# A decoder step on one core: HGRN2 projections and levels ahead of the attention projections

## What is computed

```python
h = rmsnorm(x, norm_mix)
hq, hf, hi, hg, nq, kc, vc, ks, vs, kw, vw, ngate, mgate = split(h @ w_in)
# HGRN2, 4 heads of 128: f = lb + (1-lb) sigmoid(hf), k = (1-lb) sigmoid(-hf)
#   S_t = f_t S_(t-1) + k_t hi_t ; o = silu(hq) S, rmsnorm, times silu(hg)
# attention, 8 heads of 64 in 2 groups:
#   compressed blocks of 32 rows + the rows themselves (selected) + a window
#   each with its own softmax, gated by sigmoid(ngate)
x += (sigmoid(g_a) * (a @ W_a) + sigmoid(g_b) * (b @ W_b)) @ w_out
h2 = rmsnorm(x, norm_ffn); g, u = split(h2 @ w_gate_up)
x += (gelu(causal_conv3(g)) * u) @ w_down
```

## Time and profile before

| | |
|---|---|
| runs | 1332.82 us median of 3 (1332.56 to 1334.46) |
| profiled execution | 1333.15 us |
| its span, first to last instruction | 1331.3 us |
| TensorE busy, share | 1252.7 us, 94% |
| VectorE, ScalarE, GpSimd busy | 652.9, 463.5, 152.4 us |
| mean granted TensorE clock | 0.966 of full |

### The profile page before, as it was taken

One profiled execution on the slowest core, in us unless ns is written; L12 is line 12 of the kernel. 1 busy time (PEld: TensorE's weight loads), 2 busy tenths in 40 slices (PEclk: granted clock), 3 DMA queues, 4 the chain that ended last, 5 costly groups with the idle time before them and its releaser, 6 DMA issues.

```text
span 1331.3 us, 20487 instructions
## 1 busy us (share of the span) xinstructions
PE 1252.7 (94%) x8353; PEld 1037.4 (78%) x8353; DVE 652.9 (49%) x1210; ACT 463.5 (35%) x788; POOL 152.4 (11%) x298
## 2 busy tenths in 40 slices
PE   5999988999998999999799999879999999999996
PEld 3567565667998999999765765656689989999994
DVE  3012476435755777653211225653475477676333
ACT  1120323435335444432112122243543454444220
POOL 0201032002110110100101012400021010110000
PEclk9999988998999999999999999889899999999998
DMA  7552422034944454333553342020566434433501
GB/s 228 206 157 93 128 64 64 1 96 116 291 141 127 129 180 136 106 133 125 159 193 95 127 136 85 9 56 6 172 179 223 131 123 159 158 111 128 180 1 39
DMA packets 136669, 166.01 MB, mean 125 GB/s; under 512 B 14612, under 2 KB 97334, under 8 KB 136246
## 3 DMA queue, kind: packets, MB, share of 16 engines
q1 hardware_dynamic: 136570, 164.64, 38.8%
HBM read 156.22 MB, written 12.46 MB: 127 GB/s over the span
## 4 chain that ended last, share of the span: by engine, by line
PE 87%; DVE 6%; issue 4%; ACT 2%; POOL 1%; DMA 0%; SPq 0%; POOLq 0%; DVEq 0%; PEldq 0%
PE mm L628 59%; PE ax L628 23%; PE ax L631 4%; ACT attb L1176 1%; POOL mixb L1957 1%; DVE ring_low L1728 1%; POOL mixb L1972 1%; DMA attb<-in_norm_final 0%; ACT work L1176 0%; DVE hT L1465 0%; DVE hT L1828 0%; DVE pcs L1583 0%; DVE attb L1591 0%; ACT work_parts L1176 0%; DVE xT L1873 0%
## 5 line engine op out<-in xcount | busy, mean ns | idle before, releaser
L1728 DVE TENSOR_TENSOR ring_low<-ring,work_parts 128x2048 fp32r<-128x2048 f32 (+1 forms) x96 | 207.2, 2158 | 143.7 <-ACT work_parts L1176 143.3
L628 PE MATMUL mm<-work_parts 128*128 128x320 f32 x832 | 258.4, 311 | 6.8 <-DVE h_low L1732 6.6
L628 PE MATMUL mm<-h_low,work_parts 128*128 128x320 f32 x832 | 260.0, 312 | 0.0
L628 PE MATMUL mm<-work_parts,ring_low 128*128 128x320 f32 x832 | 256.9, 309 | 0.0
L1176 ACT ACTIVATE work_parts<-ring 128x2048 fp32r<-128x2048 f32 (+1 forms) x96 | 173.7, 1810 | 159.5 <-PE mm L628 81.1
L628 PE MATMUL mm<-hT,ring 128*128 128x320 f32 (+1 forms) x896 | 216.7, 440 | 0.0
L628 PEld LDWEIGHTS mm<-hT,ring 128*128 128x128 f32 (+1 forms) x896 | 140.2, 177 | 70.2 <-issue 7.9
L628 PEld LDWEIGHTS mm<-work_parts 128*128 128x128 f32 x832 | 157.0, 189 | 11.3 <-issue 9.2
L628 PEld LDWEIGHTS mm<-work_parts,ring_low 128*128 128x128 f32 x832 | 157.4, 189 | 0.0
L628 PEld LDWEIGHTS mm<-h_low,work_parts 128*128 128x128 f32 x832 | 157.3, 189 | 0.0
L628 PE MATMUL ax<-act_parts,work_parts 128*128 128x320 f32 x544 | 125.8, 310 | 2.3 <-DVE ring_low L1728 1.6
(11 more groups left out here) (194 smaller groups left out, 1514.6 us busy)
## 6 DMA issues: line engine op xcount, KB each, us to landing
ring<-in_w_gate_up SPq DMA_DIRECT2D x44, 1024.0 KB, 6.8
ring<-in_w_in SPq DMA_DIRECT2D x12, 2048.0 KB, 8.7
ring<-in_w_in SPq DMA_DIRECT2D x18, 1024.0 KB, 7.8
ring<-in_w_down SPq DMA_DIRECT2D x6, 1536.0 KB, 7.2
ring<-in_w_out SPq DMA_DIRECT2D x4, 2048.0 KB, 13.6
ring<-in_w_down SPq DMA_DIRECT2D x4, 2048.0 KB, 8.5
ring<-in_w_down SPq DMA_DIRECT2D x4, 1280.0 KB, 5.8
ring<-in_cache_cmp_kv SPq DMA_DIRECT2D x32, 128.0 KB, 2.5
```

Of the source, the lines that this page charges most:

```text
L628: return nc.tensor.matmul(out, lhsT, rhs, start=start, stop=stop)
L1728: V.tensor_tensor(unit_of(u, ring_r), unit_of(u, ring), unit_high(u).bitcast(F32), ALU.subtract).then_inc(*st.up(w_low))
```

## The change

The HGRN2 projections `hf` and `hq` come first. The levels stand between the projections that follow: 0, 1, 2 ahead of `kvc0`, `kvc1`, `kvc2`, level 3 among the turned cached rows, 4 and 5 behind `kvn0` and `kvn1`, 6 behind `nq0`. The HGRN2 keys are turned (`krt`) ahead of the rotated queries, and the gate products (`gsel`) come behind the cached rows. The four attention units then run without levels, with the `hi` and `hg` tiles in a new order, and ScalarE and VectorE have new orders to match. The cached rows are copied by ScalarE instead of GpSimd, and into another place; `qraw` has a place of its own. GpSimd does its part of the levels first, then the rotation of the keys, and copies the samples' queries last. `BLOCKS` puts `w_hf`, `w_hq` and `w_kvc` ahead of `cmp`, so the cached rows are loaded when `par`'s slot is free, in the layer itself. Waits on counted numbers (`mm_act, 17` and the like) become waits by name.

```diff
-BLOCKS = (["par", "cmp", "w_kvc", "w_kvn", "w_nq", "w_hf", "w_hq", "w_cmp", "w_hi", "w_hg", "kv0", "mg0", "mg1", "kv1",
+BLOCKS = (["par", "w_hf", "w_hq", "w_kvc", "cmp", "w_kvn", "w_nq", "w_cmp", "w_hi", "w_hg", "kv0", "mg0", "mg1", "kv1",
...
 def mm_plan():
-    out = [(f"kvc{i}", "A") for i in range(3)] + [(f"kvn{i}", "A") for i in range(3)]
-    out += [(f"nq{m}", "A") for m in range(4)] + [(f"hf{h}", "A") for h in range(HH)]
-    out += [(f"hq{h}", "V") for h in range(HH)] + [(f"hi{i}", "A") for i in range(3)]
-    out += [(f"hg{h}", "V") for h in range(HH)]
+    out = [(f"hf{h}", "A") for h in range(HH)] + [(f"hq{h}", "V") for h in range(HH)]
+    out += [(f"kvc{i}", "A") for i in range(3)] + [(f"kvn{i}", "A") for i in range(3)]
+    out += [(f"nq{m}", "A") for m in range(4)]
+    out += [("hi0", "A"), ("hi1", "A"), ("hg0", "V"), ("hi2", "A")] + [(f"hg{h}", "V") for h in range(1, HH)]
...
 def ax_plan():
     out = [("par", "V"), ("norm1", "A"), ("cst", "V")]
-    out += [(f"cc{s}", "AV"[s % 2]) for s in range(NSEQ)]
-    out += [("cp", "A"), ("kt0", "A"), ("kt1", "V")]
+    for kk in range(3):
+        out += level_plan(kk)
+    out += [(f"cc{s}", "AV"[s % 2]) for s in range(4)] + level_plan(3)
+    out += [(f"cc{s}", "AV"[s % 2]) for s in range(4, NSEQ)] + [("cp", "A"), ("gsel0", "V"), ("gsel1", "V")]
+    for kk in range(4, len(LEVELS)):
+        out += level_plan(kk)
+    out += [("kt0", "A"), ("kt1", "V")] + [(f"krt{h}", "AV"[h % 2]) for h in range(HH)]
...
-    for n in range(4):
-        out += level_plan(2 * n)
-        out += [(f"sc{n}_{r}", "V") for r in range(GRP)] + [(f"scc{n}", "V")]
-        out += turned(n - 1) if n else []
-        out += level_plan(2 * n + 1) if 2 * n + 1 < len(LEVELS) else []
-        out += [("gsel0", "V"), ("gsel1", "V")] if n == 0 else []
-    out += [(f"krt{h}", "AV"[h % 2]) for h in range(HH)]
+    def scored(n):
+        return [(f"sc{n}_{r}", "V") for r in range(GRP)] + [(f"scc{n}", "V")]
+
+    out += scored(0) + scored(1) + turned(0) + scored(2) + turned(1) + scored(3) + turned(2)
...
-        qraw = qL
+        qraw = part(work, 7048, HH * T).rearrange("p (h t) -> p h t", h=HH)
...
-        craw = part(mixb, 7680, NCS * 512).rearrange("p (s c) -> p s c", s=NCS)
+        craw = part(mixb, 9984, NCS * 512).rearrange("p (s c) -> p s c", s=NCS)
...
             load("par", 0)
+            load("w_hf", 0)
+            sp.dma_start(cst_all[:, NFIRST:], consts[:, NFIRST:]).then_inc(consts_in, 16)
+            load("w_hq", 0)
             load("w_kvc", 0)
-            sp.dma_start(cst_all[:, NFIRST:], consts[:, NFIRST:]).then_inc(consts_in, 16)
-            load("w_kvn", 0)
             sp.wait_ge(consts_in, 32)
-            load("cmp", 0)
...
                 pe.wait_ge(*landed_at("w_hf", l))
                 w = kt_of("w_hf", KD, 512)
-                feature_tile("hf0", w, plain(w, 0))
+                for h in range(HH):
+                    feature_tile(f"hf{h}", w, plain(w, P * h), 0 if h == 0 else None)
+                pe.wait_ge(*landed_at("w_hq", l))
+                w = kt_of("w_hq", KD, 512)
+                for h in range(HH):
+                    feature_tile(f"hq{h}", w, plain(w, P * h))
+                for i in range(3):
+                    level(i)
+                    compressed_rows(i, l)
+                for q in range(4):
+                    rows_turned(q)
+                level(3)
+                for q in range(4, NCS):
+                    rows_turned(q)
+                for hb in range(2):
+                    bank = begin(AXR, f"gsel{hb}")
+                    if hb == 0:
+                        pe.wait_ge(*MM.emptied_at("kvc2"))
+                    mm(bank[:, 0:24], con("sel", SMP)[:, P * hb:P * hb + P], gts[0:SMP, 2, :], True,
+                       True).then_inc(ax_full, 1)
+                for i in range(3):
+                    keys_and_values(i, l)
+                    if i < 2:
+                        level(4 + i)
+                queries(0, l)
+                level(6)
+                queries(1, l)
+                queries(2, l)
                 for x in range(2):
                     bank = begin(AXR, f"kt{x}")
                     if x == 0:
@@ -965,16 +998,17 @@
                     for i in range(3):
                         last = tr(bank[:, P * i:P * i + TM[i]], stok[0:TM[i], i, 256 * x:256 * x + P])
                     last.then_inc(ax_full, 1)
-                for h in range(1, HH):
-                    feature_tile(f"hf{h}", w, plain(w, P * h))
+                queries(3, l)
+                pe.wait_ge(kl_ready, len(LEVELS) + 1)
+                for h in range(HH):
+                    bank = begin(AXR, f"krt{h}")
+                    for i in range(3):
+                        last = tr(bank[0:TM[i], P * i:P * i + P], kL[:, h, P * i:P * i + TM[i]])
+                    last.then_inc(ax_full, 1)
                 for m in range(4):
                     bank = begin(AXR, f"nqr{m}")
                     pe.wait_ge(qraw_ready, m + 1)
                     mm(bank[:, 0:T], con("perm"), qraw[:, m, :], True, True).then_inc(ax_full, 1)
-                pe.wait_ge(*landed_at("w_hq", l))
-                w = kt_of("w_hq", KD, 512)
-                for h in range(HH):
-                    feature_tile(f"hq{h}", w, plain(w, P * h))
...
-                for n in range(4):
-                    level(2 * n)
-                    if n == 0:
-                        pe.wait_ge(q_ready, 4)
-                        pe.wait_ge(*AXR.emptied_at("kt1"))
-                        pe.wait_ge(*AXR.emptied_at("vc2"))
-                        pe.wait_ge(kc_ready, 1)
-                    scores(n)
-                    if n == 0:
-                        hgrn_values(1, l)
-                    else:
-                        values(n - 1)
-                    if n in (1, 2):
-                        out_gate(2 * n - 2, l)
-                    if 2 * n + 1 < len(LEVELS):
-                        level(2 * n + 1)
...
-                pe.wait_ge(kl_ready, len(LEVELS) + 1)
-                for h in range(HH):
-                    bank = begin(AXR, f"krt{h}")
...
+                pe.wait_ge(q_ready, 4)
+                pe.wait_ge(*AXR.emptied_at("kt1"))
+                pe.wait_ge(*AXR.emptied_at("vc2"))
+                pe.wait_ge(kc_ready, 1)
+                scores(0)
+                hgrn_values(1, l)
+                scores(1)
+                out_gate(0, l)
+                values(0)
+                scores(2)
+                hgrn_values(2, l)
+                values(1)
+                scores(3)
+                out_gate(1, l)
+                out_gate(2, l)
+                values(2)
+                out_gate(3, l)
...
+                for h in range(HH):
...
+                for h in range(HH):
...
+                def pair_rows(q, src):
+                    A(craw[:, q, :].rearrange("p (x a d) -> p x a d", x=4, a=2),
+                      src.rearrange("p a (x d) -> p x a d", x=4), ACT.Copy).then_inc(*st.up(rows_ready))
+
+                sc.wait_ge(*landed_at("cmp", l))
+                sc.sem_inc(spare, 1)
+                for q in range(NSEQ):
+                    pair_rows(q, slot("cmp").rearrange("p (s a c) -> p s a c", s=NSEQ, a=2)[:, q])
                 for i in range(3):
                     bank = take(MM, f"kvc{i}")
                     A(gts[0:TM[i], i, :], bank[0:TM[i], 256:280], ACT.Sigmoid)
                     A(ctok[0:TM[i], i, :], bank[0:TM[i], 0:256], ACT.Copy).then_inc(*st.up(mm_act))
-                for i in range(3):
-                    bank = take(MM, f"kvn{i}")
-                    A(stok[0:TM[i], i, :], bank[0:TM[i], :], ACT.Copy).then_inc(*st.up(mm_act))
+                    if i == 1:
+                        sc.wait_ge(*st.settled())
+                        pair_rows(NSEQ, ctok[:, 0:2, :])
...
                 bank = take(AXR, "cp")
                 A(cmp_rows(NSEQ), cmp_bank(bank), ACT.Copy).then_inc(*st.up(ax_act))
+                for i in range(3):
+                    bank = take(MM, f"kvn{i}")
+                    A(stok[0:TM[i], i, :], bank[0:TM[i], :], ACT.Copy).then_inc(*st.up(mm_act))
...
-                    if h == 0:
+                    if m == 2:
                         bank = take(AXR, "kt0")
...
+                sc.wait_ge(ql_ready, len(LEVELS) + 1)
+                for h in (0, 2):
+                    bank = take(AXR, f"krt{h}")
+                    A(krP[:, h].rearrange("p i d -> p (i d)"), bank[:, 0:256], ACT.Copy)
+                    A(krS[0:SMP, h, :], bank[0:SMP, 256:384], ACT.Copy).then_inc(*st.up(ax_act))
...
-                for n, (i, g) in enumerate(UNITS):
+                def unit_exp(n):
...
                     prob, pcs, nm, sm = probs[n % 2], pcb[n % 2], nmb[n % 2], smb[n % 2]
-                    if n:
-                        turned(n - 1)
                     sc.wait_ge(max_ready, n + 1)
...
-                    if n == 0:
-                        hgrn_values(1)
```

(106 more changed lines are left out.)

190 lines of the change are left out of this document (82 added, 108 removed).

## The result

The changed kernel takes 1339.16 us (median of 15 runs, 1336.59 to 1342.1) against 1331.81 us of the kernel before (median of 15, 1327.65 to 1342.01). The ratio is 1.0055 with a 95% interval of 1.0037 to 1.0072: slower by half a per cent, where I had forecast no change. The profiled execution took 1342.1 us, 8.95 more than the profiled one of before; it is the slowest of its fifteen, while that of before lies near its median.

What follows compares the result with a forecast made beforehand. TensorE, busy 1252.7 of 1331.3 us, was taken as the bound, with time won only where it idles or runs at its lower clock. Terms -12.6 - 1.2 + 2.9 + 9.8 - 0.4 + 4.0 - 2.5 = 0.0 gave 1332.8 us, range 1321 to 1342.

Steps and rivals of the forecast that it cites:

- The rival with the clock falling in the projections and at each 1.4 us wait: Lower clock at level 0, both scores waits and level 3 in each layer: +7.9 us, 1341 us; chance 0.23.
- a stretch over 80: Sign for the slow side: first scores to first sample keys taking over 80 us, where 75.4 was forecast.
- Waits (2): Levels between projections: new TensorE waits at levels 0 and 3 and two lost covers, 4.9 us a layer, +9.8 us.
- Attention (1): Attention units without levels: the stretch falls to 75.4 us, 5.4 less in layer 0 and 7.2 in layer 1, -12.6.
- -1.2: Layer 1's level 0, at the lower clock before (2.82 us against 1.61), leaves the attention stretch: -1.2 us.
- +2.9: Charge for as many small clock slips as layer 1 had before, 1.2 and 1.7 us: +2.9 us.
- Clock at level 3 (3): A slip to the lower clock around level 3's 2.65 us idle time, 2.0 us a layer: +4.0 us.
- Rows on ScalarE (4): Cached rows copied by ScalarE and loaded within the layer: covered everywhere, nought, up to +1 us in the prologue.
- -0.4: First tile: HGRN2 matmuls of 320 columns are slower than `h` comes, the old 256 faster: -0.2 us a layer.
- The jump (5): Stall between the layers, 5.71 us, shrinks as 2 MB less are loaded there: up to 3.3 us, taken as -2.5.

Runs made afterwards that it cites:

- e1: Changed kernel with ScalarE copying unit 2's turned rows ahead of unit 3's exponentials (two lines swapped): 1327.5 us, ratio to the kernel before 0.996.
- e4: Changed kernel with the first four of eight k-steps of `hi2` and `hg1` moved ahead of the small scores of units 2 and 3: 1332.5 us, ratio 0.9991.
- e5: Changed kernel with spare products cut to fit (one, two and seven) in the waits of 1.31, 1.58 and 4.75 us: 1333.77 us, ratio 1.0013.
- e13: Changed kernel with the first three of `hi1`'s eight products moved ahead of the first scores: 1335.7 us, ratio 1.0004.
- e2: Changed kernel with VectorE making level 3's queries ahead of its row copies 1 and 3: 1336.1 us, ratio 1.0024.
- e3: Changed kernel with too many spare products (five and nine) ahead of the small scores of units 2 and 3: 1351.21 us, ratio 1.0135.
- e8: Changed kernel with the next layer's `w_hq` and `w_kvc` loads held until the jump to it is made: 1335.97 us, ratio 1.0018.
- e9: Changed kernel with the edits of e1, e2 and e4 together: 1313.87 us, ratio to the kernel before 0.9884.
- e10: Changed kernel with e1, e4 and the later levels of e6, but VectorE's row copies ahead of level 3's queries: 1310.44 us, ratio 0.9855.
- e14: e12 with e13's split of `hi1` around the first scores: 1308.1 us, ratio to the kernel before 0.9785.
- e7: Changed kernel with the eight cached rows copied on GpSimd again, ahead of its level work: 1338.14 us, ratio 1.0028.
- e6: Changed kernel with levels one tile later, row transposes ahead of level 3, and VectorE's level 3 queries ahead of its row copies: 1345.8 us, ratio 1.0083.
- e11: e9 with the `w_hq` and `w_kvc` loads held until the jump, as in e8: 1314.11 us, ratio to the kernel before 0.9876.
- e12: e10 with the `w_hq` and `w_kvc` loads held until the jump, as in e8: 1308.41 us, ratio to the kernel before 0.9841.

## Why the prediction was wrong

The forecast's sum of 0.0 stands against +8.95 us of the profiled executions and +7.35 of the medians. The rival with the clock falling in the projections and at each 1.4 us wait (1341, chance 0.23) came nearest, and its mechanism is what the runs show. That its number is so near is in part luck: of its places, level 0 never slipped (1.61 us in both layers), level 3 did in one layer and the second scores wait in one, while it left out the largest, the first scores with `hi1`, and the compressor. The sign "a stretch over 80" was met. Term by term, from the profiled executions:

- **Waits (2), +9.8: right.** 1.21, 2.51, 0.45 and 0.73 us, 4.9 a layer, in both layers. So were the waits within the stretch: 1.31 and 1.58 for 1.4 each, 4.75 for 4.7, with the cause named (`unit_exp(3)` ahead of `turned(2)`, shown by e1).
- **Attention (1), -12.6, with -1.2 and +2.9: the step that failed.** The stretch takes 82.2 and 81.5 us, not 75.4: +0.3 in both layers together for the -12.6. What is missing is passages at the lower clock: scores and `hi1` 3.3 us in layer 0 and 4.9 in layer 1, `hi2` 1.7 in both, the gate tiles 1.7 in layer 0. I charged only the one behind the long wait in the stretch itself (2.8 us a layer), and 2.9 for all "small slips". e4 and e5 show that the waits of 1.3 and 1.6 us cause theirs; e13 shows that the first comes of the cover that left: I counted level 0's leaving as a wait of 0.6 us and nothing more.
- **Clock at level 3 (3), +4.0: too much at one place and none at another.** The transposes slip in layer 0 alone, 1.5 us. The compressor's products, 7.48 us before and 9.20 now, slip in both layers, 3.4 us in all; I hadn't counted them. They stand behind 64 one-column products and a wait of 0.45. Why they slip wasn't tried and stays open; in e2, e3, e4, e8, e9 and e10 those of layer 1 took 7.51, and in e14 those of layer 0.
- **Rows on ScalarE (4), 0: nothing against it** (e7). The -0.4 at the first tile can't be read apart.
- **The jump (5), -2.5: wrong by 3.** The stall went from 5.71 to 6.26. I took the traffic to be much smaller, since 2 MB less are loaded there; `w_kvc` alone is still issued just as the engines stop. It has landed two microseconds before they start, so that the stall before the change ended as traffic ended was no proof of my reason. A link there is: with `w_hq` and `w_kvc` held the idle time is 5.2 to 5.8 us (three pairs), 1.7 to 2.4 less and not the 3.3 I allowed.

The rest, some 5.5 us less than before, is passages at the norms and behind the units that neither kernel's edits touch, such as the final norm (7.49 us before, 4.58 after). That last one is chance of the execution: in e1 the same norm took 7.48. The waits came within 0.2 us a layer of the forecast (12.5 for 12.4). The lower clock was priced at 12.5 us in both layers together (2.8 and 2.0 a layer, and 2.9) and took 12.9 in layer 0 and 10.7 in layer 1, the compressor's open 3.4 among them. These 11.1 us more and the 3.0 of the jump, less the 5.5, account for 8.6 of the 8.95 us. I priced most waits at their length, and taken together they cost nearly twice that.

The Trainium skill ("TensorE: Matmul & The Clock Gate", "What's actually happening") has recent activity opening the gate. The trace agrees: spare products alone, whose results are thrown away, bring `hi2` from 8.78 to 7.08 us. I gave this rule 0.23 because ten products had run at the full clock behind a wait of 0.72 us. They still do in e1 and e5. But one row behind one wait was no evidence for waits of twice the length amid small scores, nor for one behind 36 short products.

The Trainium skill ("Runtime: NRT & Kernel Launch", "Instruction fetch mechanics") has a taken branch out of the loaded pages wait for a fetch before anything runs. That fits the 5.2 us that stay with the loads held; no run here shows the fetch itself.

## What to carry to other kernels

Price a wait of TensorE as its length and the passage behind it, with a chance: here 1.31 us of wait had 1.7 us of lower clock behind it in 12 of 14 cases, 1.58 in 7 of 14, 4.75 had 2.3 to 3.2 in all, and the 1.21 ahead of level 0 had none. When work is moved out of a stretch, look at which small waits it covered there, and put the halves of a large tile, not the whole of it, on both sides of each; that split and one swap each on ScalarE and VectorE turned 0.5% slower than before into 1.2% faster (e9). Ahead of moving an instruction that waits, list what stands behind it on its engine (5.33 us in e6).

## What was unexpected

- Spare products made the kernel faster: 1.07, 1.34 and 3.93 us of them a layer, put into waits, took 5.4 us off the median (e5).
- A won passage can reappear at the next small wait (e13), so the rows of one execution can promise more than the medians show. Twelve runs of that one program spread over 13.5 us, from 1328.06 at a mean granted clock of 0.978 to 1341.61 at 0.967.
- The stall at the jump depends on which loads were issued ahead of it: 7.1 to 7.8 us of idle time in the changed kernel and the ten runs with `w_hq` and `w_kvc` issued ahead of it, 5.05 to 5.8 in the four with both held (e8, e11, e12, e14).
- VectorE's product of 1280 columns takes 3.60 us for 1.49 in e6, where GpSimd's of the same size (2.91 us) began 0.7 us earlier: the mechanism of the earlier trace rows, at another place.
